# One tile lags three rows and three norms change who adds their squares, in a transformer kernel that keeps TensorE busy

## What is computed

```python
def rmsnorm(x, g):
    y = x * lax.rsqrt(jnp.mean(x * x, axis=-1, keepdims=True) + EPS)
    return y * g

# first block, layer l (l = 0, 1)
h = rmsnorm(x, g_pre_mix[l])
(c_q, c_kv, k_r, p_in, s_u, s_v, ...) = split_cols(h @ w_in[l])
merged = ...                                      # four branches, gated
x = x + rmsnorm(merged @ w_out[l], g_post_mix[l])
h = rmsnorm(x, g_pre_ffn[l])
f = (silu(h @ w_ffn_gate[l]) * (h @ w_ffn_up[l])) @ w_ffn_down[l]
x = x + rmsnorm(f, g_post_ffn[l])

# second block: mod = silu(c) @ w_mod + b_mod, split in shifts, scales and gates
x = x + g1 * (y @ w_o)                            # y: two branches, gated
h2 = modulate(rmsnorm_2(x, norm2_g), sh2, sc2)    # the middle norm of block 2
x = x + g2 * swiglu(h2, w_ffn_gate, w_ffn_up, w_ffn_down)
```

## Time and profile before

| | |
|---|---|
| time, median of 3 runs | 2526.13 us (2524.79 to 2532.34) |
| time of the profiled execution | 2527.75 us |
| its span | 2525.8 us |
| TensorE busy | 2491.9 us, 99% of the span |
| GpSimd busy | 1809.6 us, 72% |
| VectorE busy | 1163.1 us, 46% |
| ScalarE busy | 586.2 us, 23% |
| chain that ended last | TensorE 91%, VectorE 3%, issue 2%, GpSimd 2% |
| mean granted clock of TensorE | 0.994 of full |

### The profile page before, as it was taken

The page is one execution under the profiler, slowest core; times in us unless marked ns, Lnnn a source line. Parts: engine busy times, 40 slices in busy tenths (PEclk is TensorE's granted clock), DMA queues, the critical chain, the costliest instruction groups (busy, mean ns, idle before and its releaser), DMA issues.

```text
span 2525.8 us, 33949 instructions
## 1 busy us (share of the span) xinstructions
PE 2491.9 (99%) x11988; PEld 2028.2 (80%) x11988; DVE 1163.1 (46%) x1677; ACT 586.2 (23%) x1021; POOL 1809.6 (72%) x832
## 2 busy tenths in 40 slices
PE   9999999999999999999999999999999999999999
PEld 6878788788888787878878888878887787888887
DVE  7764423544454776442354445665237725511100
ACT  3243312311110323331231111132324522211100
POOL 7766678888888576677788888835452467688887
PEclk9999999999999999999999999999999999999999
DMA  4222223223355222222232335511122222223333
GB/s 144 90 84 83 86 89 100 75 92 99 115 201 188 71 92 84 83 83 92 97 106 97 100 109 199 184 43 59 43 67 84 75 77 91 83 94 97 99 113 104
DMA packets 70210, 250.86 MB, mean 99 GB/s; under 512 B 8304, under 2 KB 8432, under 8 KB 70000
## 3 DMA queue, kind: packets, MB, share of 16 engines
q1 hardware_dynamic: 66528, 239.69, 28.8%
q10 hardware_dynamic: 3600, 9.99, 1.1%
HBM read 247.56 MB, written 2.10 MB: 99 GB/s over the span
## 4 chain that ended last, share of the span: by engine, by line
PE 91%; DVE 3%; issue 2%; POOL 2%; DMA 1%; ACT 1%; SPq 0%; POOLq 0%; DVEq 0%; ACTq 0%
PE bank L511 23%; PE bank L507 23%; PE bank L508 23%; PE bank L448 4%; PE bank L450 4%; PE bank L449 4%; PE bank L874 1%; PE bank L1240 1%; POOL w_hi L404 1%; PE bank L899 1%; PE bank L883 1%; PE bank L1224 1%; POOL w_lo L407 1%; PE bank L1214 1%; DMA w_raw<-weights 0%
## 5 line engine op out<-in xcount | busy, mean ns | idle before, releaser
L404 POOL TENSOR_TENSOR w_hi<-w_raw,one 128x1024 fp32r<-128x1024 f32 x405 | 781.3, 1929 | 672.7 <-PE bank L511 456.8
L407 POOL TENSOR_TENSOR w_lo<-w_raw,w_hi 128x1024 fp32r<-128x1024 f32 x405 | 1009.7, 2493 | 31.7
L507 PE MATMUL bank<-act_hi,w_hi 128*128 128x512 f32 x1792 | 708.1, 395 | 5.8 <-POOL w_hi L404 2.9
L508 PE MATMUL bank<-act_lo,w_hi 128*128 128x512 f32 x1792 | 698.0, 389 | 0.0
L511 PE MATMUL bank<-act_hi,w_lo 128*128 128x512 f32 x1856 | 462.4, 390 | 0.0
L511 PEld LDWEIGHTS bank<-act_hi,w_lo 128*128 128x128 f32 x1856 | 348.3, 188 | 73.2 <-issue 1.0
L507 PEld LDWEIGHTS bank<-act_hi,w_hi 128*128 128x128 f32 x1792 | 336.4, 188 | 83.2 <-issue 12.4
L508 PEld LDWEIGHTS bank<-act_lo,w_hi 128*128 128x128 f32 x1792 | 336.6, 188 | 72.9 <-issue 4.3
L507 PE MATMUL bank<-f_hi,w_hi 128*128 128x512 f32 x528 | 207.2, 392 | 2.0 <-POOL w_hi L404 2.0
L508 PE MATMUL bank<-f_lo,w_hi 128*128 128x512 f32 x528 | 205.6, 389 | 0.0
L511 PE MATMUL bank<-f_hi,w_lo 128*128 128x512 f32 x528 | 131.8, 390 | 0.0
(11 more groups left out here) (477 smaller groups left out, 3598.5 us busy)
## 6 DMA issues: line engine op xcount, KB each, us to landing
w_raw<-weights SPq DMA_DIRECT2D x405, 512.0 KB, 3.5
mod_raw<-mods SPq DMA_DIRECT2D x48, 512.0 KB, 4.3
bias<-bias ACTq DMA_DIRECT2D x8, 512.0 KB, 4.9
resid<-x SPq DMA_DIRECT2D x8, 256.0 KB, 5.4
out<-resid ACTq DMA_DIRECT2D x8, 256.0 KB, 4.3
params<-params ACTq DMA_DIRECT2D x2, 534.5 KB, 4.0
ctx_raw<-ctx ACTq DMA_DIRECT2D x1, 1024.0 KB, 7.0
second<-second ACTq DMA_DIRECT2D x1, 972.5 KB, 10.2
```

The source lines that it names most:

```text
L404: nc.gpsimd.tensor_tensor(w_hi[:, j, :], w_raw[:, j, :], one[:, 0:1].to_broadcast([P, 1024]), ALU.mult)\
L407: nc.gpsimd.tensor_tensor(w_lo[:, j, :], w_raw[:, j, :], w_hi[:, j, :].bitcast(F32), ALU.subtract).then_inc(blocks_split, 1)
L507: mm(out, w_hi[:, slot, tile * P:tile * P + P], rows_hi, start=start, stop=False)
L508: mm(out, w_hi[:, slot, tile * P:tile * P + P], rows_lo, start=False, stop=False)
```

## The change

1. **Feed-forward start, layers 0 and 1.** Tile 0 takes the rows as they become ready, tile 1 follows three rows behind. The single ones product moves from within tile 3 to tile 2, between its matmuls with `w_hi` and those with `w_lo`.
2. **Layer border.** The eight ones products go. ScalarE squares into `row_squares`, VectorE adds up (`squares_total`, accumulating in bank 7), and one ones product stands within the third latent tile. The second latent tile lags three rows. Of the modulation sums, four stand ahead of `y_norm_spread`, then come two warm products and four sums, and three sums follow each row.
3. **First tiles of a layer.** The second tile of `p_in` reads the raw rows; VectorE scales it when it is read out (ScalarE copied it before). The first tile of `s_u` (u == 6) is now the first to read the normed rows, and the sums of squares of the latents follow it. `apply` has two banks in place of three, and the first tile of `p_in` is in bank 4 in place of bank 0.
4. **Block 2, middle norm.** ScalarE's squares stay. VectorE adds rows 0 to 6 up in bank 5 (`square_added`), one add per output tile. The seven ones products after the output tiles and the one in `first_from_raw` become two in `first_from_raw`: of the added rows and of row 7.

```diff
--- before.py
+++ after.py
@@ -21,6 +21,7 @@
+EARLY_BANK[4] = 4
@@ -31,7 +32,7 @@
-NORM_BANK = (4, 5, 7)
+NORM_BANK = (5, 7)
@@ -290,6 +291,8 @@
+        square_acc = bank[5][:, :]
@@ -477,10 +480,10 @@
-            def keep_warm(n):
+            def keep_warm(n, b=5):
...
-                    mm(bank[5][:, :], ones, rope, start=True, stop=True)
+                    mm(bank[b][:, :], ones, rope, start=True, stop=True)
@@ -492,7 +495,17 @@
-            def x_norm_from_squares(n):
+            def x_norm_added(n):
+                pe.wait_ge(x_summed, 8 * n + KT - 1 + 2)
+                mm(bank[7][:, :], ones, sum_sq, start=True, stop=False)
+            def x_norm_rest(n):
+                pe.wait_ge(x_sq, 8 * n + len(SQUARED_BY_ACT))
+                mm(bank[7][:, :], ones, squares[(KT - 1) % 2], start=False, stop=True).then_inc(x_summed, 1)
+            def x_norm_total(n):
@@ -510,7 +523,8 @@
-            def block_product(b, out, slot, rows_hi, rows_lo, ks, start=True, stop=True, norm=None, each=None):
+            def block_product(b, out, slot, rows_hi, rows_lo, ks, start=True, stop=True, norm=None, each=None,
+                              amid=None):
@@ -520,18 +534,16 @@
+                if amid is not None:
+                    amid()
...
-            def full_each(b, out, slot, each):
-                block_product(b, out, slot, act_hi, act_lo, range(KT), each=each)
-            def full(b, out, slot, rows=(act_hi, act_lo)):
-                block_product(b, out, slot, rows[0], rows[1], range(KT))
+            def full(b, out, slot, rows=(act_hi, act_lo), amid=None):
+                block_product(b, out, slot, rows[0], rows[1], range(KT), amid=amid)
@@ -603,7 +615,8 @@
-                        x_norm_sum(2 * DEPTH + 1, KT - 1)
+                        x_norm_added(2 * DEPTH + 1)
+                        x_norm_rest(2 * DEPTH + 1)
@@ -622,11 +635,26 @@
-                    first_two(b0, [bank[0][:, :], bank[1][:, :]], lo0, odd)
-                    pairs(0, (2,))
-                    free(3, ordinal(3))
-                    full_each(b0 + 3, bank[3][:, :], (3 + odd) % 2,
-                              lambda k: x_norm_from_squares(norm) if k == 3 else None)
+                    take(b0)
+                    take(b0 + 1)
+                    def gate_up_part(j, k):
+                        last = product(bank[j][:, :], (j + odd) % 2, k, act_hi[:, k, :], act_lo[:, k, :], k == 0,
+                                       k == KT - 1)
+                        if k == KT - 1:
+                            last.then_inc(blocks_done, 1)
+                    behind = 3
+                    for k in range(KT):
+                        pe.wait_ge(lo_ready, lo0 + k + 1)
+                        gate_up_part(0, k)
+                        if k >= behind:
+                            gate_up_part(1, k - behind)
+                    for k in range(KT - behind, KT):
+                        gate_up_part(1, k)
+                    free(2, ordinal(2))
+                    full(b0 + 2, bank[2][:, :], odd, amid=lambda: x_norm_total(norm))
+                    pairs(0, (3,))
@@ -743,7 +769,8 @@
-                full(BL * l + B_CQ + 2, early_bank(2)[:, :], (B_CQ + 2) % 2, (raw_hi, raw_lo))
+                full(BL * l + B_CQ + 2, early_bank(2)[:, :], (B_CQ + 2) % 2, (raw_hi, raw_lo),
+                     (lambda: x_norm_total(2 * l)) if l > 0 else None)
@@ -754,7 +781,7 @@
-                    if u == 5:
+                    if u == 6:
@@ -766,8 +793,8 @@
-                        full(BL * l + b, early_bank(u)[:, :], b % 2, (raw_hi, raw_lo) if u == 4 else (act_hi, act_lo))
-                    if u == 5:
+                        full(BL * l + b, early_bank(u)[:, :], b % 2, (raw_hi, raw_lo) if u < 6 else (act_hi, act_lo))
+                    if u == 6:
@@ -911,23 +938,31 @@
-                    mod_sums(0, 7)
+                    mod_sums(0, 4)
...
-                    mod_sums(7, 15)
+                    keep_warm(2, 4)
+                    mod_sums(4, 4)
...
-                    outs = [bank[0][:, :], bank[1][:, :]]
...
+                    def latent_part(j, k):
+                        last = product(bank[j][:, :], (B_CQ + j) % 2, k, raw_hi[:, k, :], raw_lo[:, k, :], k == 0,
+                                       k == KT - 1)
+                        if k == KT - 1:
+                            last.then_inc(blocks_done, 1)
+                    behind = 3
...
-                        x_norm_sum(2 * l + 2, k)
...
-                        for j in range(2):
-                            last = product(outs[j], (B_CQ + j) % 2, k, raw_hi[:, k, :], raw_lo[:, k, :], k == 0, k == KT - 1)
-                            if k == KT - 1:
-                                last.then_inc(blocks_done, 1)
-                        mod_sums(22 + k, 1)
-                    mod_sums(30, 2).then_inc(mods_done, 1)
+                        latent_part(0, k)
+                        if k >= behind:
+                            latent_part(1, k - behind)
+                        last = mod_sums(8 + 3 * k, 3)
+                    last.then_inc(mods_done, 1)
+                    for k in range(KT - behind, KT):
+                        latent_part(1, k)
@@ -1321,8 +1356,7 @@
-            w_out(DEPTH, B2_OUT, use_2, merge_2, B2_OUT % 2,
-                  then=lambda m: x_norm_sum(2 * DEPTH + 1, m - 1) if m > 0 else None)
+            w_out(DEPTH, B2_OUT, use_2, merge_2, B2_OUT % 2)
@@ -1380,7 +1414,7 @@
-                    run(act_hi[:, k, :], bank[NORM_BANK[k % 3]][:, :], ACT.Copy).then_inc(hi_ready, 1)
+                    run(act_hi[:, k, :], bank[NORM_BANK[k % 2]][:, :], ACT.Copy).then_inc(hi_ready, 1)
@@ -1458,9 +1492,6 @@
-                for u in (5,):
-                    act.wait_ge(blocks_done, BL * l + B_PIN[u - 4] + 1)
-                    run(pin[:, u - 4, 16:], bank[EARLY_BANK[u]][:, :], ACT.Copy).then_inc(bank_free[EARLY_BANK[u]], 1)
@@ -1561,8 +1592,7 @@
-                        act.wait_ge(x_summed, 8 * (2 * l + 2) + k + 1)
-                        run(squares[k % 2], resid[:, k, :], ACT.Square).then_inc(x_sq, 1)
+                        run(row_squares[:, k, :], resid[:, k, :], ACT.Square).then_inc(x_sq, 1)
@@ -1820,12 +1850,12 @@
-                    v.tensor_tensor(act_lo[:, k, :], bank[NORM_BANK[k % 3]][:, :], act_hi[:, k, :].bitcast(F32),
+                    v.tensor_tensor(act_lo[:, k, :], bank[NORM_BANK[k % 2]][:, :], act_hi[:, k, :].bitcast(F32),
...
-                    if k >= 3:
-                        dve.wait_ge(lo_ready, 16 * l + k - 2)
-                    v.scalar_tensor_tensor(bank[NORM_BANK[k % 3]][:, :], resid[:, k, :], g_pre[:, k:k + 1], bank[6][:, :],
+                    if k >= 2:
+                        dve.wait_ge(lo_ready, 16 * l + k - 1)
+                    v.scalar_tensor_tensor(bank[NORM_BANK[k % 2]][:, :], resid[:, k, :], g_pre[:, k:k + 1], bank[6][:, :],
@@ -1838,14 +1868,14 @@
-            def squares_added(n):
+            def squares_total(n, acc):
...
-                    v.tensor_tensor(row_squares[:, KT - 2, :] if k == KT - 1 else bank[6][:, :],
-                                    row_squares[:, 0, :] if k == 1 else bank[6][:, :], row_squares[:, k, :],
+                    v.tensor_tensor(row_squares[:, KT - 2, :] if k == KT - 1 else acc,
+                                    row_squares[:, 0, :] if k == 1 else acc, row_squares[:, k, :],
@@ -2046,6 +2076,9 @@
+                dve.wait_ge(blocks_done, BL * l + B_PIN[1] + 1)
+                v.tensor_tensor(pin[:, 1, 16:], bank[EARLY_BANK[5]][:, :], rstd_row, ALU.mult)\
+                    .then_inc(bank_free[EARLY_BANK[5]], 1)
@@ -2241,7 +2274,7 @@
-                squares_added(2 * l + 1)
+                squares_total(2 * l + 1, bank[6][:, :])
@@ -2265,6 +2298,7 @@
+                    squares_total(2 * l + 2, bank[7][:, :])
@@ -2536,6 +2570,23 @@
+            def square_added(k):
+                if k == KT - 1:
+                    return
+                dve.wait_ge(x_sq, 8 * (2 * DEPTH + 1) + k + 1 - KT + len(SQUARED_BY_ACT))
+                if k == 0:
+                    v.tensor_copy(square_acc, squares[0]).then_inc(x_summed, 1)
+                else:
+                    dve.wait_ge(x_summed, 8 * (2 * DEPTH + 1) + k + 2)
+                    v.tensor_tensor(sum_sq if k == KT - 2 else square_acc, square_acc, squares[k % 2], ALU.add)\
+                        .then_inc(x_summed, 1)
+            def out_row(k):
+                raw_low_2(k)
+                square_added(k)
@@ -2579,7 +2630,7 @@
-            add_gated(B2_OUT, 1, M_GATE1, "out", raw_low_2)
+            add_gated(B2_OUT, 1, M_GATE1, "out", out_row)
```

4 lines of the change are left out of this document (1 added, 3 removed).

## The result

| | before | changed |
|---|---|---|
| median | 2531.44 us (2524.79 to 2539.04, 8 runs) | 2520.24 us (2513.96 to 2524.34, 8 runs) |
| profiled execution, its span | 2527.75, 2525.8 us | 2513.96, 2512.2 us |

The ratio is 0.9959, 95% interval 0.9946 to 0.9972: faster by 0.41%, 10.4 us by the ratio. The forecast was 2513.8 us, the range 2510.5 to 2519.5. The time of the kernel before, 2526.13 us, was a median of three runs; eight give 2531.44, and the 29 beside the first experiments 2529.77. The two profiled executions lie 13.8 us apart, more than the medians do.

A forecast was written before the change was run, and what follows sets the result against it. TensorE, busy 99% of the span, was taken as the bound. Gains of 4.2 (block 2), 2.4 (feed-forward starts) and 5.7 us (layer border) make 12.3, so 2526.1 - 12.3 = 2513.8 us; range 2510.5 to 2519.5.

The forecast's parts named there:

- Block 2: Middle norm: seven ones products leave w_out, two stand in first_from_raw; gain 4.2 us, bounds 3.5 to 5.1.
- 0.26 us late: Block 2, w_out: VectorE stays some 0.26 us behind TensorE's tiles, which lengthens the wait at the end.
- Feed-forward starts: Layers 0 and 1: earlier ones product removes the wait ahead of tile 4; 1.2 us each, 2.4 in all.
- Layer border: Ones products go, rows come 2.14 us apart, third latent tile starts earlier; gain 5.7 us.
- the case that I took: Layer border: clock falls at about 818.5 us, row 0 starts at 823.8, end at 842.0; 5.7 us, against 6.4 at full clock.
- the base: Whole kernel: the median before the change, 2526.13 us, from which the forecast gain of 12.3 us was taken.
- In layer 0 nothing of this is waited for: First tiles of layer 0: the later normed rows and VectorE's extra work make TensorE wait for nothing; no cost.
- Rival A: Clock falls in the new gaps at the border and feed-forward starts; one fall 2516 to 2517.6 us, all 2523.5; chance 0.20.
- B: Border rows still come at 2.46 us, waiting replaces ones products, feed-forward starts give nothing; 2518.6 us; chance 0.08.
- C: Block 2: GpSimd holds VectorE's new add, banks come late, 18 us; 2531.6 us; chance 0.04.
- D: Layer 1: VectorE's chain gives back up to 3 us of the border's gain; 2517 us; chance 0.07.

The follow-up runs named there:

- the 29 beside the first experiments: 29 runs, not a run numbered 29: the kernel before, unchanged, run again beside the first set of follow-up kernels; median 2529.77 us.
- p5: Kernel before with tile 1 of the feed-forward starts three rows behind, the ones product left in tile 3; ratio 1.0005 to the kernel before.
- p6: Kernel before with the feed-forward starts' ones product in tile 2, tiles 0 and 1 together row by row; ratio 0.9979 to the kernel before.
- v2: Changed kernel with more 512-column warm products in the layer border's waiting time and its sums spread differently; ratio 0.9952 to the kernel before.
- v3: Changed kernel with v2's border, block 2's banks 2 and 3 waited for late, feed-forward tiles 0 and 1 together, layer 0's sums after tile 5; 2512.25 us.
- v4: v3 with half of the latents' one-column sums behind tile 6 and half behind tile 7, in both layers; 2513.92 us.

## Why the prediction was partly right

**Block 2:** 4.2 us forecast, 4.4 measured in all eight traces with it and bank 3 waited for up front. VectorE was not 0.26 us late; the rest is as written.

**Feed-forward starts:** 1.2 us each forecast, 1.5 and 1.4 measured where the clock stays. The mechanism is right to 0.1 us at each tile. The lag had no part in the gain (p5, p6).

**Layer border:** 5.7 us forecast, 6.0 measured in the case that I took (half clock at the start), on every point: rows 2.14 us apart, row 0 at 823.7 (823.8), third tile at 841.9 (842.0). Three of seven traces were not this case.

**What failed, the base:** "its differences are taken off the median, 2526.13 us". Three runs gave a base that eight put 5.3 us higher. The same difference taken off 2531.44 gives 2519.1, and the measured 2520.24 would lie well inside a range moved by 5.3 us. I had counted nothing in the range for the base, though the three runs shown lay 7.5 us apart, and the profiled trace had the sums of layer 1 at full clock, which most of its kind have not.

**What failed in the sum:** "In layer 0 nothing of this is waited for", which put layer 0's first tiles and all behind them at nothing. No wait arose at the norm, but the sums now stand later in time, and with that went 1.6 us of half clock; and TensorE's program is another, and with that went some 1.7 us at 710 us. In layer 1, with the new place of the sums, about 1 us comes back.

**Rival A** was given 0.20, priced at 2.1 us for a border and 3.8 for a start. It came about in three of seven borders, at 2.5 to 8.4 us, and in six of 20 starts, at 0.5 or 2.2. The forecast took it as not there; in the mean of the seven it costs 2.4 us at the border. The Trainium skill (TensorE: Matmul & The Clock Gate, section Why this matters for your kernels) warns of idle gaps between bursts of matmuls. The border's falls come behind gaps, though short ones, none over 0.8 us. The fall behind the sums of layer 0 does not agree: TensorE was busy without a gap, at one-column matmuls. **B, C, D** did not come: rows at 2.14, adds at 0.68, no new wait for VectorE in layer 1.

By the means of the places, new order against old: -4.4 for block 2, -2.2 for the starts, -4.3 for the border (of the nine old borders four lose 1.6 too), then +1.6 for the first tiles of layer 0, +1.7 at 710 us and -1.0 for those of layer 1 make 8.6 us. 1650 to 1920 us adds 2.6, 11.2 in all, against 10.4 measured. Of the 2.6, 1.06 are the wait at 1724 us that is gone, and the other 1.5 are stretches at half clock. What decides when the clock falls stays open, there and everywhere. It is luck that the difference, 12.3 forecast, came this near: losses of 3.3 us that I didn't have stand against gains of 3.6 that I didn't have either.

## What to carry to other kernels

When a kernel's time moves by a few us from run to run, forecast a difference and give the base a range of its own, from the spread of the runs. Look for TensorE's one-column matmuls and for rows in which it mostly waits: 512-column products in the waiting time kept the clock in three traces of three. Splitting up the one-column sums may do so too; one trace speaks for it. When two edits come together, try each without the other: here the lag brought no gain, and all six falls at a start came with it.

## Not expected of the hardware

- One product of one column more in TensorE's program moved a packet of kind instruction by 9 us, 270 us later, and with it a wait of 0.39 us became one of 1.70.
- The same 24 one-column matmuls cost 0 or 1.6 us, and what goes with it is the microsecond at which they stand: in layer 0 none of eight traces lost it with the sums at 48.1 to 50.7 us, all of 11 with them at 52.0 to 56.2.
- A stretch at half clock is not dear by its length: 6.8 us of it over the border's waiting time cost 1.0 us (6.0 gained against 7.0 in v2, v3 and v4, which kept the clock), 10.2 us over its rows 3.5.
